# The first two jobs of a two-block transformer kernel, fed in turns of half a job

## The reference

```python
h = rms_norm(x, norm1_g[l])            # x * rsqrt(mean(x*x) + eps) * g
z = h @ w_in[l]
glu_in, q, k, v, gate_logits = jnp.split(z, SPLITS, axis=-1)
a_val, a_gate = jnp.split(glu_in, 2, axis=-1)
a = a_val * jax.nn.sigmoid(a_gate)     # 1024 channels
a = causal_depthwise_conv(a, conv_w[l], conv_b[l])   # 31 taps
a = jax.nn.silu(rms_norm(a, conv_norm_g[l]))
y_a = a @ w_conv_out[l]
...                                    # attention over q, k, v in three dilations
x = x + (g_a * y_a + g_b * y_b) @ w_out[l]
...                                    # gated feed-forward part, then the second block
```

## Time and profile before

| what | us |
|---|---|
| median of three runs | 829.8 |
| the profiled execution, its own time | 830.39 |
| its span | 828.6 |
| PE busy | 817.7 (99% of the span) |
| DVE busy | 649.0 (78%) |
| ACT busy | 555.5 (67%) |
| POOL busy | 229.2 (28%) |

### The profile page before, as it was taken

How to read it: one execution, slowest core, us unless ns; L and a number is a source line. 1 busy time by engine, 2 the same in 40 slices (tenths; PEclk the granted TensorE clock), 3 DMA queues, 4 the chain that set the end, 5 groups by cost and what they waited for, 6 DMA issues and landing times.

```text
span 828.6 us, 16588 instructions
## 1 busy us (share of the span) xinstructions
PE 817.7 (99%) x6010; PEld 764.3 (92%) x6010; DVE 649.0 (78%) x1171; ACT 555.5 (67%) x1023; POOL 229.2 (28%) x245
## 2 busy tenths in 40 slices
PE   9999999999999999999999999999999999999996
PEld 9998998999999999999889979999998988888886
DVE  7998989997979998787766968856689866666552
ACT  8777999996756776666455775486647665655442
POOL 0387852333322244433101000020022333322110
PEclk9999999999999999999999999999999999999999
DMA  7666554446466477665756544435345575565741
GB/s 271 217 197 195 178 180 135 160 141 204 151 202 182 129 226 207 182 193 164 233 170 206 159 172 136 153 121 179 127 144 191 180 209 194 182 199 166 233 135 51
DMA packets 43168, 146.12 MB, mean 176 GB/s; under 512 B 4928, under 2 KB 7632, under 8 KB 43088
## 3 DMA queue, kind: packets, MB, share of 16 engines
q1 hardware_dynamic: 42192, 144.13, 55.3%
q10 hardware_dynamic: 896, 0.94, 0.4%
HBM read 144.00 MB, written 1.05 MB: 175 GB/s over the span
## 4 chain that ended last, share of the span: by engine, by line
PE 86%; DVE 5%; ACT 4%; issue 2%; DMA 1%; SPq 0%; DVEq 0%; ACTq 0%
PE px L561 20%; PE px L565 16%; PE px L566 16%; PE px L567 16%; PE px L562 10%; DVE wlo L1463 2%; DMA raw<-ws 1%; ACT whi L941 1%; PE px L572 1%; PE px L571 1%; PE px L573 1%; PE px L638 1%; DVE hx L1731 1%; PE px L650 1%; PE px L787 1%
## 5 line engine op out<-in xcount | busy, mean ns | idle before, releaser
L1463 DVE TENSOR_TENSOR wlo<-raw,whi 128x1024 fp32r<-128x1024 f32 x265 | 331.1, 1256 | 28.8 <-ACT whi L941 28.8
L941 ACT ACTIVATE whi<-raw 128x1024 fp32r<-128x1024 f32 x265 | 278.4, 1053 | 52.5 <-PE px L562 24.5
L565 PE MATMUL px<-hx,whi 128*128 128x256 f32 x1024 | 292.7, 286 | 0.8 <-DVE hx L1480 0.3
L566 PE MATMUL px<-hx,whi 128*128 128x256 f32 x1024 | 285.8, 279 | 0.0
L567 PE MATMUL px<-hx,wlo 128*128 128x256 f32 x1024 | 285.7, 279 | 0.0
L565 PEld LDWEIGHTS px<-hx,whi 128*128 128x128 f32 x1024 | 192.5, 188 | 4.4 <-issue 1.6
L566 PEld LDWEIGHTS px<-hx,whi 128*128 128x128 f32 x1024 | 192.6, 188 | 0.5
L567 PEld LDWEIGHTS px<-hx,wlo 128*128 128x128 f32 x1024 | 192.5, 188 | 0.0
L2104 POOL TENSOR_TENSOR CA<-CA,ct 128x256 f32<-128x256 f32 x90 | 90.2, 1002 | 96.8 <-DVE wlo L1463 76.4
L561 PE MATMUL px<-fx,whi 128*128 128x512 f32 x330 | 114.5, 390 | 0.0
L561 PE MATMUL px<-hx,whi 128*128 128x512 f32 x320 | 111.1, 390 | 0.1
(11 more groups left out here) (330 smaller groups left out, 1321.6 us busy)
## 6 DMA issues: line engine op xcount, KB each, us to landing
raw<-ws SPq DMA_DIRECT2D x265, 512.0 KB, 3.6
tb<-tabs SPq DMA_DIRECT2D x16, 128.0 KB, 3.5
X<-xs SPq DMA_DIRECT2D x4, 256.0 KB, 3.9
raw<-ws SPq DMA_DIRECT2D x3, 256.0 KB, 5.7
out<-Y SPq DMA_DIRECT2D x1, 384.0 KB, 2.4
vc<-vecs SPq DMA_DIRECT2D x1, 315.5 KB, 7.0
raw<-ws ACTq DMA_DIRECT2D x1, 256.0 KB, 3.9
msk<-lmask ACTq DMA_DIRECT2D x1, 256.0 KB, 2.9
```

The source lines that it names most:

```text
L565: e.matmul(b[:, 0:S], H, xh, start=first, stop=False)
L566: e.matmul(b[:, 0:S], H, xl, start=False, stop=False)
L941: e.activation(whi[:, n % NSL, :], raw[:, n % NRAW, :], ACT.Copy).then_inc(s_hi, 1)
L1463: e.tensor_tensor(wlo[:, n % NSL, :], raw[:, n % NRAW, :], whi[:, n % NSL, :], ALU.subtract).then_inc(s_lo, 1)
```

## The change

The time-critical opening is written in another order.

- **Loads.** SP issues the input tiles and the half chunks in turns: X 0, weights (0, 0), X 1, weights (1, 0), X 2, weights (0, 1), X 3, weights (1, 1), where (c, h) is half h of chunk c. Chunk 2 is loaded in halves too. ACT issues no weight load any more. The load of the remaining vectors now stands behind chunk 3.
- **PE.** Job `ag` 0 does its blocks 0 to 3, then `av` 0 its blocks 0 to 3, then `ag` 0 its blocks 4 to 7, then `av` 0 the same. There are 10 multiplications by ones before it, not 16. The sum of squares stands in the middle of job `av` 1 and no more behind `av` 0: 28 blocks precede it, not 16.
- **Jobs without 1 / rms.** Eight and not six (`EARLY` = 4), so `hx` is first wanted in chunk 8 and no more in chunk 6.
- **ACT and DVE.** The splits of the halves stand between the `ax` tiles in the same turns. The splits of chunks 3, 4 and 5 now come before 1 / rms; those of chunks 6 to 9 stand in the list behind it. The first tanh of ACT stands behind three tiles of `hx` and not two.
- **Taps.** They begin in chunk 8 and no more in chunk 6. The quota is 3.2 from the start (2.2 up to chunk 11 before) on DVE, and 2.2 (2.0 before) on POOL. The total is equal again on DVE by chunk 12; the DVE's last chain ends in chunk 55 (54 before), POOL's in chunk 53 (54 before).

```diff
-HALVED = 2
-WARM = 16
-EARLY = 3
+HALVED = 3
+HALF_ORDER = ((0, 0), (1, 0), (0, 1), (1, 1), (2, 0), (2, 1))
+WARM = 10
+EARLY = 4
...
-        quota = (2.2 if c < 12 else 3.2 if c < 24 else 2.6 if c < 34 else 3.7, 2.0 if c < 34 else 1.8)
+        quota = (3.2 if c < 24 else 2.6 if c < 34 else 3.7, 2.2 if c < 34 else 1.8)
...
-            for i in range(EARLY):
-                job(("ag", i), AX, first_scaled if i == 0 else None, rings=(FEW,))
+            for tiles in (range(0, 4), range(4, KD)):
+                job(("ag", 0), AX, first_scaled, rings=(FEW,), tiles=tiles)
+                job(("av", 0), AX, rings=(SMALL,), tiles=tiles)
+            job(("ag", 1), AX, rings=(FEW,))
+            job(("av", 1), AX, rings=(SMALL,), tiles=range(0, 4))
+            sums("n1", VALUES)
+            job(("av", 1), AX, tiles=range(4, KD))
+            for i in range(2, EARLY):
+                job(("ag", i), AX, rings=(FEW,))
                 job(("av", i), AX, rings=(SMALL,))
-                if i == 0:
-                    sums("n1", VALUES)
...
-            e.dma_start(raw[:, 0, half(0)], ws[0][:, half(0)]).then_inc(s_half[0], 16)
...
             for i in range(2, KD, 2):
                 e.activation(sq[:, i - 2:i, :], X[:, i:i + 2, :], ACT.Square).then_inc(s_sq, 1)
-            highs(3)
+                if i == 2:
+                    highs(3)
+            highs(5)
             rms("n1", D)
-            highs(4)
-            for i in range(2):
+            highs(6)
+            for i in range(3):
                 first_high(i)
             early_gate(0)
...
-            tiles(0)
-            tiles(1)
-            tiles(2)
-            tiles(3)
-            half_load(0, 1)
-            half_load(1, 0)
-            half_load(1, 1)
-            loads(2)
+            for i in range(4):
+                tiles(i)
+                half_load(*HALF_ORDER[i])
+            half_load(2, 0)
+            half_load(2, 1)
+            loads(3)
```

More of the change, by code:

```diff
@@ L461, in two_blocks @@
         FROM = norm_counts()
-        LOW = {c: (s_lo, c + 1 + min(c + 1, HALVED)) for c in range(n_chunks)}
-        HI = [c + 1 + min(c + 1, HALVED) for c in range(n_chunks)]
+        HALF = {nh: k + 1 for k, nh in enumerate(HALF_ORDER)}
+        HI = [HALF[c, 1] if c < HALVED else c + 1 + HALVED for c in range(n_chunks)]
+        LOW = {c: (s_lo, HI[c]) for c in range(n_chunks)}
         def half(h):
@@ L539, in take, with job @@
                 return px[b]
-            def job(key, xs, ready=None, rings=None):
+            def job(key, xs, ready=None, rings=None, tiles=None):
                 kt, at_, w = WHERE[key]
                 rings = rings or (JOBS, JOBS)
-                banks = [take((key, t), rings[t]) for t in range(1 if w == 1 else 2)]
-                for k in range(kt):
+                tiles = tiles or range(kt)
+                if tiles[0] == 0:
+                    banks = [take((key, t), rings[t]) for t in range(1 if w == 1 else 2)]
+                else:
+                    banks = [px_of[key, t] for t in range(1 if w == 1 else 2)]
+                for k in tiles:
                     if ready:
@@ L551, in job @@
                     if c < HALVED and o in (0, CW // 2):
-                        e.wait_ge(s_lo, 2 * c + 1 + (o > 0))
+                        e.wait_ge(s_lo, HALF[c, int(o > 0)])
                     elif c >= HALVED and c != seen[0]:
@@ L988, in _ @@
                 e.activation(ax[:, i, 0, :], X[:, i, :], ACT.Copy, scale=vec("norm1_g", i)).then_inc(s_xgh, 1)
[L989 to L994, removed]
+                if i % 2:
+                    half_high(*HALF_ORDER[i // 2])
+            half_high(2, 0)
+            half_high(2, 1)
             e.activation(sqa[:, :, :], X[:, 0:2, :], ACT.Square).then_inc(s_sq, 1)
@@ L1002, in early_gate @@
                 e.wait_ge(*BANK[("ag", i), 0])
-                e.activation(sg[:, i, :], sg[:, i, :], ACT.Tanh, scale=0.5).then_inc(s_eg, 1)
+                e.activation(sg[:, i % 3, :], sg[:, i % 3, :], ACT.Tanh, scale=0.5).then_inc(s_eg, 1)
             def first_high(i):
@@ L1007, in first_high @@
                 e.activation(hx[:, i, 0, :], sq[:, nt_slot("n1", i), :], ACT.Copy).then_inc(s_nhi, 1)
-            highs(4)
-            for i in range(2):
+            highs(6)
+            for i in range(3):
                 first_high(i)
             early_gate(0)
-            first_high(2)
-            highs(5)
+            highs(7)
             for i in (3, 4):
@@ L1017, in _ @@
             early_gate(1)
-            highs(6)
             first_high(5)
-            highs(7)
+            highs(8)
             for i in (6, 7):
@@ L1023, in _ @@
             early_gate(2)
+            highs(9)
+            early_gate(3)
             def products(c):
@@ L1451, in half_low @@
             def half_low(n, h):
-                e.wait_ge(s_hi, 2 * n + h + 1)
+                e.wait_ge(s_hi, HALF[n, h])
                 e.tensor_tensor(wlo[:, n, half(h)], raw[:, n, half(h)], whi[:, n, half(h)], ALU.subtract).then_inc(s_lo, 1)
@@ L1503, in _ @@
                                        op0=ALU.mult, op1=ALU.subtract).then_inc(s_xgl, 1)
[L1504 to L1509, removed]
+                if i % 2:
+                    half_low(*HALF_ORDER[i // 2])
+            half_low(2, 0)
+            half_low(2, 1)
             for i in range(3):
+                if i == 1:
+                    lows(3)
                 e.wait_ge(s_sq, i + 2)
@@ L1514, in _ @@
                 e.tensor_tensor(sqa[:, :, :], sqa[:, :, :], sq[:, 2 * i:2 * i + 2, :], ALU.add).then_inc(s_add, 1)
-            lows(3)
+            lows(5)
             def early(key, to):
@@ L1524, in early_gated @@
                 e.wait_ge(*BANK[("av", i), 0])
-                e.scalar_tensor_tensor(out=CI[:, i, 30:], in0=sg[:, i, :], scalar=1.0, in1=CI[:, i, 30:], op0=ALU.add,
+                e.scalar_tensor_tensor(out=CI[:, i, 30:], in0=sg[:, i % 3, :], scalar=1.0, in1=CI[:, i, 30:], op0=ALU.add,
                                        op1=ALU.mult).then_inc(s_ci, 1)
@@ L1536, in _ @@
             early(("av", 0), CI[:, 0, 30:])
-            first_tiles((0, 1), ())
-            first_tiles((2,), (0, 1))
-            lows(4)
+            first_tiles((0, 1, 2), (0, 1))
             early(("ag", 1), sg[:, 1, :])
             early_gated(0)
+            lows(6)
             first_tiles((3, 4), (2, 3))
-            lows(5)
             early(("av", 1), CI[:, 1, 30:])
-            first_tiles((5,), (4,))
             early_gated(1)
+            lows(7)
             early(("ag", 2), sg[:, 2, :])
-            lows(6)
-            first_tiles((6, 7), (5, 6, 7))
-            lows(7)
+            first_tiles((5, 6, 7), (4,))
+            lows(8)
+            first_tiles((), (5, 6, 7))
+            early(("av", 2), CI[:, 2, 30:])
+            early_gated(2)
+            e.wait_ge(s_ci, 1)
+            early(("ag", 3), sg[:, 0, :])
             e.wait_ge(s_vc, 16)
@@ L1555, in _ @@
             e.tensor_scalar(qg8[:, :], vec("qg"), -0.125, None, ALU.mult).then_inc(s_cst, 1)
-            early(("av", 2), CI[:, 2, 30:])
-            early_gated(2)
+            lows(9)
+            early(("av", 3), CI[:, 3, 30:])
+            early_gated(3)
             def taps(c):
```

## The result

The changed kernel takes **837.53 us** (median of 5 runs, 836.64 to 839.22) against 830.48 us for the kernel before, measured beside it (829.62 to 831.78): ratio 1.0084, 95% interval 1.0074 to 1.0095. It is slower by 7 us. The forecast was 830.5 and its range ended at 832.3, so it was wrong in size and in kind. The profiled execution is 837.77 us with a span of 835.9, 7.3 more than before.

What follows compares the result with a forecast made beforehand. PE, busy 817.7 of 828.6 us, was taken as the bound, with DVE's list limiting the opening. PE reaching chunk 9 0.7 us later, added to the median 829.8, gave 830.5 us; range 828.3 to 832.3.

Steps and rivals of the forecast that it cites:

- both waits on ACT: DVE's list behind 1 / rms: 1.15 us at the first joined tile for tanh, 0.4 us at chunk 8's split.
- The slow half rate behind the pause: Opening: PE's half rate outlasts the pause from 5.3 to 6.0 us, 1.3 us on top, 831.8 us; chance 0.23.
- late halves: Opening: weight halves land no sooner, 0.8 to 1.2 us more in 1 / rms and at chunk 9, 831.5 us; chance 0.10.
- 0.7 us: Opening: PE reaches chunk 9 later by 0.3 to 0.8 us, taken as 0.7 us, and keeps that lag from chunk 10.
- DVE's stop of 0.51 us: DVE's list at 29.76 us in the kernel before, cause not shown; might come again or not, 0 or 0.5 us less.
- the upper of my two sums: DVE's list from 1 / rms to the end of chunk 9's split: 16.4 us, against 15.9 without the last item.
- From chunk 10 on I expect the kernel before, shifted: Everything behind the opening: the kernel runs as before, only 0.7 us later.
- Taps two chunks later with a higher quota are covered by that: Behind chunk 9: DVE's 5.0 us per chunk pair against PE's 5.6 covers the taps; uncovered, a tap more is 0.4 us.
- POOL ends earlier: End of the taps: POOL finishes its taps earlier than before; no size given.
- 2 us stay: DVE's last tap moves one chunk, some 3 us behind 195.1 us; PE wants it at 200.2 us, leaving 2 us.
- side gain: Later in the kernel: a gain such as the 0.6 us wait at 143 us going, 829 us; chance 0.05.
- early start stays: Opening: PE's earlier start is kept through chunk 9, 1.45 us won, 828.35 us; chance 0.17.

Runs made afterwards that it cites:

- 1.0 tap a chunk: Changed kernel with early tanh table, POOL 2.0 taps, exact waits, DVE 3.75, earlier chunk 9 split, old bank turn; POOL 1.0 in chunks 38 to 42, then 2.4: 831.79 us.
- the run at 2.0: Changed kernel with only POOL's quota set to 2.0 taps a chunk throughout, instead of 2.2 then 1.8: 834.14 us.
- The plan alone: Kernel before with only the tap plan changed: chains start behind chunk 7, 3.2 and 2.2 taps a chunk: 833.32 us.
- the early table load: Changed kernel; ACT loads tanh's table right behind 1 / rms and splits chunk 6 later, DVE scales tiles 3 and 4 before chunk 6's split: 835.55 us.
- the banks: Changed kernel with only the turn of the PSUM banks put back to where it stood with three early pairs: 836.2 us.
- POOL's early start: Changed kernel at 2.2 taps, POOL's adds started sooner by reordering ACT's products and DVE's tap weights and dropping POOL's waits in chunks 8 and 9: 836.79 us.

## Why the prediction was wrong

**The opening.** Right as a mechanism: start, both waits on ACT, PE's waits at chunks 7 to 9, place by place. The slow half rate behind the pause did not come (records 0.12 us apart from 6.13 us on), nor did late halves. That was partly luck: in this execution the records of the ones stand 0.12 us apart already from 4.56 us on, ahead of the pause. Over the 17 traces this sets in anywhere between 3.9 and 7.1 us, and in one with 10 multiplications (that with 1.0 tap a chunk) only at 6.75 us, 0.8 us behind the first block, so that rival can occur, there for three records and 0.3 us. Mis-sized: 0.7 us was 1.33. The 0.3 us by which chunk 2 was late stay through the sum and 1 / rms; 0.15 come on top at chunk 9 and 0.1 at chunk 10. DVE's stop of 0.51 us did not come again, but three handovers of 0.1 us did; its list took 16.52 us (18.94 to 35.46), the upper of my two sums. The row of before that it is held against was itself at the late end: in four other executions of that opening chunk 2 starts between 14.09 and 14.44 us, not at 14.63.

**The step that failed** is "From chunk 10 on I expect the kernel before, shifted", with its grounds "Taps two chunks later with a higher quota are covered by that" and "POOL ends earlier". I asked whether DVE had room for more taps. It had. I didn't ask POOL, which from 34.35 to 76.40 us is busy 36.77 us and has gaps only between its adds (0.17 us at most behind the second), nor what an add costs beside a split, nor who waits for POOL: ACT, whose list is in order, and which has 1.1 us of idle time from 76 to 143 us. From chunk 10 to the scores the lag grows by 4.09 - 1.33 = 2.8 us; in the run at 2.0 it grows by 0.15. The plan alone makes the kernel before 2.6 us slower.

**"2 us stay"** at the last tap was right in that PE doesn't wait for the tap itself: it ends at 201.47 us, and PE begins the third job `ao` at 205.83. But it moved from ahead of a split to behind it, and so moved the low part of an `ao` tile. With the 0.3 us at 179 us, which goes with the same edit of the quota, that is 0.6 to 0.7 us.

**What I did not look for.** The bank that a job uses is set by a turn counter, and a job moved from one ring to another moves all that follow. The forecast went by the order of instructions, in which the names of the banks are left out; 0.7 us.

**The place of the 0.6 us wait at 143 us.** I listed it as a side gain. It is a second bound of the kernel: ACT's list. The one lead that a run brought there, 0.44 us, was lost whole, so I doubt that the "early start stays" case (0.17) could have been reached; a lead of 1.45 us was not run.

**What stays open.** The last 1.5 us of the lag, between 490 and 502 us. ACT waits for a load there:

```profile
499.87 1.06 ACT L953 ACTIVATE whi<-raw 128x1024 fp32r<-128x1024 f32 x1 [3.01 <-DMA raw<-ws]
```

The same wait was 0.60 us in the kernel before and 0.78 with 2.0 taps. ACT's next piece is then 7.24 us late (500.83 for 493.59), which is PE's lag from 502 us on. Between 490 and 520 us the executions lose between -0.4 and 2.6 us against the one of before, without an order that I can see in the edits, and the runs at 2.0 and with the early table load owe part of their gain to it. I did not test what decides when this load lands. Four traces (the plan alone, the table load, the banks, POOL's early start) lose another 0.96 us between 290 and 390 us, evenly spread and without a wait; that is open too.

## What to carry to other kernels

When a change shifts work on a side engine, compare the rate asked of it per stage with its time per item in that stage (one by one, since a mean hides items that another engine holds up), and then ask which in-order engine waits for it and whether that one has any idle time in the stage behind; the bound may be two engines away from the busy one. Before an early start is priced, look for the first later place where the main engine already waits: whatever is won ahead of it only makes that wait longer. And where buffers go by turns, compare buffer numbers too, not only the order.

## What the runs showed of the hardware

**A slower clock behind a short wait.** In the profiled execution of the run with 1.0 tap a chunk PE waited 1.31 us at 503.73; behind that the granted clock was 0.52 from 505 to 507 us and 0.75 to 510, which is the level of 1.2 GHz and then a mix with 2.4, and the records stood 0.21 us apart, not 0.12, until 508.5. That lost another 1.5 us. Length, PE's busy us (records), clock, DMA share and GB/s:

```profile
501.00:503.00 2.00, 1.41 (x12) 1.00 0.77 227
503.00:504.00 1.00, 0.27 (x5) 1.00 0.95 356
504.00:505.00 1.00, 1.00 (x18) 1.00 0.22 86
505.00:507.00 2.00, 2.00 (x11) 0.52 0.42 39
507.00:510.00 3.00, 3.00 (x21) 0.75 0.41 154
```

In the changed kernel a wait of 1.32 us in front of the same instructions (509.16) left the clock at 1.00:

```profile
506.00:509.00 3.00, 1.84 (x16) 1.00 0.87 276
509.00:511.00 2.00, 1.84 (x22) 1.00 0.21 84
```

In none of the other 16 traces does the clock fall between 8 and 819 us. So the fall is one case behind a wait of 1.3 us, and that the wait brought it is not shown. The Trainium skill, page "TensorE: Matmul & The Clock Gate", Part 1, says that "the default state is throttled, and activity releases the throttle". Both levels show in the first trace; the second shows that a wait of this length need not bring the lower one back.

**GpSimd's adds stand still while a split of VectorE runs.** 0.74 us alone or beside taps, 1.5 to 1.9 us if a split (a subtraction of two tiles in SBUF, 128x1024) runs or starts within 0.1 us, and then the add ends 0.6 us behind the split. In the first 30 adds of the kernel before, of the changed one and of the one at 2.0 taps (90 in all) there is no exception.

**A wait for a bank has no name.** Twice the trace gave "issue" for a wait whose cause the experiments name or bear out: the bank at the third `ao` (gone with the turn of the banks), and the head sum at 87.35, which goes when ACT's `hsq` comes in time (POOL at 2.0 taps).
